# Prompt attention: from two query tiles of one head to one query tile of two heads

## The reference, cut to what matters

```python
p_c = masked_softmax(einsum('bqkgd,bnkd->bqkgn', q, kc) * scale, m_c)     # compressed keys, 63 of them
o_c = einsum('bqkgn,bnkd->bqkgd', p_c, vc)
p_s = masked_softmax(einsum('bqkgd,bkqmd->bqkgm', q, ks) * scale, m_s)    # selected: all tokens up to the query
o_s = einsum('bqkgm,bqkmd->bqkgd', p_s, vs)
p_w = masked_softmax(einsum('bqkgd,bwkd->bqkgw', q, kw) * scale, m_w)     # window: the last 512 tokens
o_w = einsum('bqkgw,bwkd->bqkgd', p_w, vw)
return gates[..., 0:1] * o_c + gates[..., 1:2] * o_s + gates[..., 2:3] * o_w
```

## Time and profile before

| | |
|---|---|
| time, median of 3 runs | 1833.09 us (1832.91 to 1834.04) |
| the profiled execution | 1833.64 us |
| its span from first to last instruction | 1831.9 us |
| granted TensorE clock, mean | 0.996 |
| PE / DVE / ACT / POOL busy | 98% / 64% / 51% / 25% of the span |

### The profile page before, as it was taken

How to read it: one execution, slowest core, us unless ns; L and a number is a source line. 1 busy time by engine, 2 the same in 40 slices (tenths; PEclk the granted TensorE clock), 3 DMA queues, 4 the chain that set the end, 5 groups by cost and what they waited for, 6 DMA issues and landing times.

```text
span 1831.9 us, 32124 instructions
## 1 busy us (share of the span) xinstructions
PE 1804.1 (98%) x11818; PEld 1618.9 (88%) x11819; DVE 1181.5 (64%) x1673; ACT 934.2 (51%) x1574; POOL 460.3 (25%) x627
## 2 busy tenths in 40 slices
PE   8999999999999999999999999999999999999998
PEld 8999999789999978999989999998768888888884
DVE  5744434566131279999999999645486686645756
ACT  4334343103021178888998888311133675545746
POOL 0000000000000016555555554002112444422431
PEclk9999999999999999999999999999999999999999
DMA  5233334314241550000000000525257797876875
GB/s 185 87 100 115 110 93 159 91 35 140 81 134 50 178 163 1 1 2 1 1 2 2 1 1 13 185 70 175 92 198 280 290 392 291 292 272 221 324 238 196
DMA packets 119762, 241.08 MB, mean 132 GB/s; under 512 B 27986, under 2 KB 84858, under 8 KB 113466
## 3 DMA queue, kind: packets, MB, share of 16 engines
q1 hardware_dynamic: 112666, 214.26, 33.4%
q0 software_dynamic: 6976, 25.17, 5.5%
HBM read 193.52 MB, written 45.88 MB: 131 GB/s over the span
## 4 chain that ended last, share of the span: by engine, by line
PE 57%; DVE 3%; ACT 2%; issue 1%; DMA 0%; POOL 0%; POOLq 0%; ACTq 0%; DVEq 0%
PE ps L3734 20%; PE ps L2191 7%; PE ps L2165 7%; PE ps L3316 4%; PE ps L263 4%; PE ps L2134 3%; PE ps L2136 3%; PE ps L3722 1%; PE ps L2126 1%; PE ps L3783 1%; PE ps L2210 1%; PE ps L2107 1%; PE ps L3728 1%; ACT region_w L2549 1%; PE ps L3793 0%
## 5 line engine op out<-in xcount | busy, mean ns | idle before, releaser
L2362 DVE TENSOR_REDUCE small<-ps 128x1 f32<-128x640 f32 (+7 forms) x256 | 176.3, 698 | 10.5 <-PE ps L2126 7.6
L2395 DVE TENSOR_TENSOR turned_low<-ps,turned_high 128x512 fp32r<-128x512 f32 (+2 forms) x304 | 178.0, 608 | 6.2 <-ACT turned_high L2562 4.5
L2562 ACT CAST turned_high<-ps 128x512 fp32r<-128x512 f32 (+2 forms) x304 | 155.4, 533 | 15.5 <-PE ps L2165 12.0
L2702 POOL TENSOR_SCALAR region_w<-region_w,small,gates 128x640 f32<-128x640 f32 (+7 forms) x172 | 138.4, 814 | 94.2 <-DVE small L2368 94.2
L2191 PE MATMUL ps<-turned_high,value_stacks 128*128 128x256 f32 (+1 forms) x608 | 159.2, 292 | 0.5 <-DVE turned_low L2395 0.5
L2191 PE MATMUL ps<-turned_low,value_stacks 128*128 128x256 f32 (+1 forms) x608 | 147.9, 281 | 0.0
L2134 PE MATMUL ps<-key_stacks,query_stacks 128*128 128x256 f32 (+3 forms) x384 | 141.0, 367 | 3.3 <-ACT region_w L2549 2.8
L3734 PE MATMUL ps<-down_parts,hidden_parts 128*128 128x512 f32 x552 | 131.1, 393 | 0.0
L2549 ACT ACTIVATE region_w<-ps,small 128x640 f32<-128x640 f32 (+7 forms) x172 | 121.2, 707 | 17.2 <-PE ps L2165 8.7
L3734 PE MATMUL ps<-up_parts,rows_parts 128*128 128x512 f32 x552 | 129.0, 389 | 0.1
L3734 PE MATMUL ps<-gate_parts,rows_parts 128*128 128x512 f32 x528 | 125.9, 394 | 0.0
(11 more groups left out here) (556 smaller groups left out, 4888.4 us busy)
## 6 DMA issues: line engine op xcount, KB each, us to landing
region_k<-in_w_gate SPq DMA_DIRECT2D x16, 2048.0 KB, 9.6
region_k<-in_w_up SPq DMA_DIRECT2D x16, 2048.0 KB, 10.9
region_w<-in_w_down SPq DMA_DIRECT2D x16, 2048.0 KB, 14.1
region_w<-in_w_in SPq DMA_DIRECT2D x14, 512.0 KB, 4.6
region_k<-in_w_in SPq DMA_DIRECT2D x10, 512.0 KB, 4.4
small<-gate_a SPq DMA_DIRECT2D x8, 516.0 KB, 3.5
region_w<-gate_b SPq DMA_DIRECT2D x8, 516.0 KB, 3.8
region_k<-in_x_prompt SPq DMA_DIRECT2D x8, 512.0 KB, 7.4
```

Of the source, the lines that this page charges most:

```text
L2362: nc.vector.tensor_reduce(nmax[:, n % 4:n % 4 + 1], sc, AX.X, ALU.max, negate=True).then_inc(s_max, 1)
L2395: nc.vector.tensor_tensor(lo, m.ps[:, turn_bank(G), 0:w], hi, ALU.subtract).then_inc(s_lo, 1)
L2562: nc.scalar.copy(hi, m.ps[:, turn_bank(G), 0:w]).then_inc(s_hi, 1)
L2702: nc.gpsimd.tensor_scalar(probs(H, t), probs(H, t), rec[:, H % 4, t:t + 1], m.gates[:, 2 * p + t, col:col + 1], ALU.mult, ALU.mult).then_i ...
```

## The change

A unit is now one query tile of two neighbouring heads 2J and 2J+1. The halves (u, g, a) stay 128, four to a unit, and the two jobs of a half are the two heads. Both have the same tile and so the same blocks; `runs`, `value`, `alone_ahead`, `first_value` and `ALONE_AHEAD` go, and `values` multiplies 256 columns for each block. A pass of the loop covers two heads, 8 units and 32 halves, and the tiles come in the order 0, 4, 1, 5, 2, 6, 3, 7. The queries of a unit, and its outputs in `RO`, are two pieces of 128 columns, 1032 columns apart. A compressed set is now two units (two tiles of two heads); both parts of its scores come behind the second job of the first of them; its clamps are needed in the sets with tile 0 alone, one in four instead of one in two. The gates are read accordingly. Buffers are laid out for the new widths. All four engines' orders are written out anew, for 32 halves per pass, so that all steps stand at other distances from each other than before. The unused `keep_awake` of this function goes.

```diff
-def queries_at(p, j):
-    return slice(j * NTOK + p * 256, j * NTOK + (p + 1) * 256), slice(p * 256, (p + 1) * 256)
+TILE_OF = (0, 4, 1, 5, 2, 6, 3, 7)
+def queries_of(x, u):
+    j, i = 2 * (u // TT), TILE_OF[u % TT]
+    return x.rearrange("p (j n) -> p j n", n=NTOK)[:, j:j + 2, i * P:(i + 1) * P]
+def two_heads(x):
+    return x.rearrange("p (t n) -> p t n", t=2)
+def query_slot(u):
+    return slice(u % 4 * 256, (u % 4 + 1) * 256)
...
-    NU = TT // 2 * NKV
-    NH2 = 2 * NU
-    NHALF = QPK * NH2
-    SCALED_BEHIND = (0, 7)
-    ALONE_AHEAD = (9, 10, 11, 12, 13, 14)
+    UNITS = QPK // 2 * TT
+    NHP = 4 * TT
+    NHALF = 4 * UNITS
+    SCALED_BEHIND = ((0, 1), (9, 1), (16, 1), (24, 1))
...
+    def tile_of(H):
+        return TILE_OF[H // 4 % TT]
+    def first_block(H):
+        return 0 if H % 2 == 0 else max(0, tile_of(H) - WBLK)
     def blocks(H):
-        j, p, g, a = half(H)
-        return [(b, t) for b in range(2 * p + 2) for t in range(2) if first_block(a, 2 * p + t) <= b <= 2 * p + t]
+        return [(b, t) for b in range(first_block(H), tile_of(H) + 1) for t in range(2)]
...
+    def clamped(c):
+        return TILE_OF.index(0) // 2 == c % (TT // 2)
...
-            for r, n in runs(H):
+            out = m.ps[:, 7, g * 256:(g + 1) * 256]
+            for n in range(width(H) // P):
                 for x in range(2):
-                    if (H, r, x) not in alone_ahead(H):
-                        last = value(H, r, x, n)
+                    last = nc.tensor.matmul(out, vs[:, a, g, first_block(H) + n, :], m.pt_parts[a][x][:, n * 256:(n + 1) * 256],
+                                            start=(a == 0 and n == 0 and x == 0), stop=False, skip_group_check=True)
...
-        for j in range(-1, QPK + 1):
-            at, c = NH2 * j, 2 * j
...
+        for j in range(-1, QPK // 2 + 1):
+            at, c = NHP * j, TT // 2 * j
+            scores(at + 8, 1)
...
+            turn(at + 33, 0)
+            scores(at + 36, 1)
+            turn(at + 34, 0)
+            values(at + 32)
+            scores(at + 37, 0)
+            values(at + 33)
+            scores(at + 37, 1)
+            scores(at + 38, 0)
+            turn(at + 35, 0)
+            values(at + 34)
+            turn(at + 36, 0)
...
```

More of the change, by code:

```diff
@@ L2073, in turned @@
         w = min(4, len(blocks(what)) - 4 * c) * P
[L2074 removed]
+        hi, lo = m.pt_parts[half(what)[2]]
         return w, hi[:, c * 512:c * 512 + w], lo[:, c * 512:c * 512 + w]
@@ L2147, in turn @@
             G = g_of[what, c]
-            between = alone_ahead(what - 1) if c == 2 and what != "C" else ()
             if what == "C":
@@ new lines, in _ @@
+            scores(at + 27, 0)
+            scores(at + 27, 1)
+            turn(at + 24, 1)
+            turn("C", c + 3)
+            values(at + 23)
+            scores(at + 28, 0)
+            turn(at + 25, 0)
+            turn(at + 25, 1)
+            scores(at + 28, 1)
+            turn(at + 26, 0)
+            values(at + 24)
+            turn(at + 26, 1)
+            scores(at + 29, 0)
+            values(at + 25)
+            scores(at + 29, 1)
+            turn(at + 27, 0)
+            turn(at + 27, 1)
@@ new lines, in _ @@
+            scores(at + 30, 0)
+            values(at + 26)
+            scores(at + 30, 1)
+            turn(at + 28, 0)
+            turn(at + 28, 1)
+            turn(at + 28, 2)
+            scores(at + 31, 0)
+            values(at + 27)
+            turn(at + 28, 3)
+            turn(at + 29, 0)
+            scores(at + 31, 1)
+            turn(at + 29, 1)
+            turn(at + 29, 2)
+            values(at + 28)
+            scores(at + 32, 0)
+            scores(at + 32, 1)
+            turn(at + 30, 0)
@@ L2315, in _ @@
+            scores(at + 39, 0)
+            values(at + 35)
+            turn(at + 36, 2)
+            scores(at + 39, 1)
+            turn(at + 37, 0)
+            scores(at + 40, 0)
     @block.vector
```

840 lines of the change are left out of this document (532 added, 308 removed).

## The result

The changed kernel takes 1836.7 us (median; 1834.6 to 1838.8) beside 1834.0 (1832.0 to 1835.9) for the kernel before: ratio 1.0013, interval 1.0007 to 1.0019. It is slower by 0.13%, with the interval clear of 1, and so within the 0.2% that the prediction called no change. The profiled execution has a span of 1835.0 us, where before had 1831.9.

A forecast was written before the change was run, and what follows sets the result against it. TensorE was taken to bound the attention stage, VectorE close behind. Values -8.6 us and new waits +3.6 us make -5.0: 1828.6 us profiled, 1828.1 us as median from 1833.1; range 1819 to 1837.

The forecast's parts named there:

- The values: TensorE's value matmuls: 320 narrow ones (128 columns) become 160 wide ones (256 columns), four narrow 0.34 us against two wide 0.236, saving 8.4 to 8.6 us.
- second rival: Nothing gained: columns alone set matmul price, or VectorE replaces TensorE as bound; 1830 to 1836 us, middle 1833; chance 0.25.
- VectorE's share: In mid prompt attention VectorE works 91 to 94% of the stage, 2 to 3 us of 58 behind TensorE.
- The new waits: Rewritten orders make TensorE wait for late engines between tiles 4 and 5: 0.9 us x 4 passes, 3.6 us lost.
- the walk: Both written orders summed beside each other, TensorE never waiting: none late before; after, worst 0.86 us at scores of half 39.
- The bound from the rows: Limits for TensorE's waits in the attention loop: -14 us if the old ones vanished, +14 if they doubled.
- The start: First units of the attention stage, with waits and lower clock: zero change, with 2 us to either side.
- The end: Last unit of the attention stage has 16, 10, 16, 10 blocks instead of 15, 10, 15, 10: under 1 us.
- The third: Rival: too little TensorE cover between small and large tiles, 16 times at 1 us each; slower, 1840 us; chance 0.1.
- The first rival: Equal work per unit removes old waits too: 1817.5 us if half go, 1821 if a quarter; chance 0.2.

## Why the prediction was wrong

Forecast 1828.1, range 1819 to 1837, measured 1836.7: the range holds it by 0.3 us, the forecast is 8.6 off, and the likeliest sign (faster, 0.55) was wrong; "same" had 0.34.

**The values: priced too low.** -8.6 us was priced; the distances give about 3.3 us a pass, some 13, and the run with the narrow ones back is 11.6 us longer. The step behind it took 0.17 us for a narrow pair "with what follows" and missed that a wide value matmul behind it takes 0.17 as well: 0.112 each, not 0.086. Of the 4.2 us a pass that this gives, transposes that had been cheaper beside value matmuls take 1.0 back. The half of the second rival by which columns alone set the price is refuted.

**VectorE's share: wrong.** 91 to 94% was worked out by taking 0.08 us of overlap off nearly every row and by shortest spacings. With the narrow matmuls left out it works 98.7% of a pass of 113.5, which is 97% of before's. Part of what was counted as cover is not there: in the trace of before, where a VectorE row waits for the one ahead of it, it starts some 0.03 us behind that one's end and not 0.08 ahead of it; with the waits for other engines the gaps add up to 5 us a pass. The engine was not 2 to 3 us of 58 behind TensorE but about level with it. How much that caps is shown by the same run: 8.0 us off TensorE gave 2.2. Of the 3.3 sought here it would have left about a quarter, if the rest of the sequence had stayed as it was; this figure is in proportion only, and was not measured.

**The new waits: the step that failed.** 3.6 us was charged for all four passes, 0.9 a pass at one late place. Measured are about 3.6 us in each pass, some 14 in four. The kind and the unit were right: in the unit of tile 4, a bank that ScalarE has not read. The place was off by one half: the longest wait, 0.80 us, is at half 38, and half 39, for which 0.86 was forecast, has 0.42. But the walk charged one place and dropped the others behind it, as though one shift cured them. The waits view has 17 of them in 3.5 passes, with 0.71 at half 46. The bound from the rows, +14 for doubled waits, was the better estimate. Why one wait is followed by others, I can only argue: a wait of TensorE makes the exponential behind its transposes late too, and so frees the next bank late. That the orders are the cause is shown by the rearrangement: the same units and work without most of these waits, 11.2 us faster. But the old units gained 6.9 us in the same way, and with the same narrow matmuls and orders of their own the new units stay 1.7 us a pass behind the old ones, so a part may belong to the units.

**The start: 1.7 us instead of 0 +- 2** in the first pass, from the lower clock, inside its bounds. Filling the gaps shows it. The end: 11.49 for 11.39 us from the last job to the last value and 0.53 for 0.30 us to the next stage, as small as said.

**The sum with the measured terms:** -13.2 + 14.4 + 1.4 (what the first pass loses beyond a steady one) + 0.1 = +2.7 us for the stage, beside +2.8 read from its ends and +2.7 between the medians. Against the forecast of -5.0 the waits are 10.8 us too many, and the values saved 4.6 us more than priced: that the time came out within the range owes something to luck, as these two errors oppose each other. The other 0.9 us of the 8.6 is the time before, 1833.1 in three executions and 1834.0 in seventeen.

**The rivals.** The second is the one that came true in what it would show: the pass still at 115.8 (116.0), with more waits for the other engines, 1836.7 against its 1830 to 1836. Its reason, VectorE in TensorE's place, is only half of it: with a fifth off VectorE's load after still has 115.0. The third, thin cover between a small and a large tile, has its place right: the longest waits are in the units of tiles 4 and 5. Its price was near as well, 4 us a pass for 3.6 measured, and its 1840 missed because the values brought more. The waits stand in front of scores, though, not of the first transposes. The first rival (old waits go too, 1817.5 to 1821) failed in the written orders; rearranged, the kernel comes nearer to it, 1825.5. VectorE's share was to rise by a point and fell by 1.4.

**What to carry over.** When two engines are nearly level, as here, a saving on one is worth little more than the distance to the other (8.0 us off TensorE gave 2.2), and that distance has to be measured by taking the work away, not by adding shortest spacings. When a change rewrites an in-order schedule, price the schedule first: here rearranging was worth 11.2 us in the new units and 6.9 in the old, and the wide matmuls 11.6. When waits are charged to the instruction ahead of them, take them out before reading what work was saved. Charge every late place of a walk until a second walk, with the first waits put in, shows that the later ones vanish.

## What was not expected of the hardware

- A 128-column matmul with its own weight load costs 0.112 us in a run of value matmuls and a 256-column one 0.118. The pair shows as 0.06 and 0.11, and the rest is in the row behind it (0.17 for 0.12), so a spacing must be read up to the second row behind a change of width.
- Behind a wait of 1.2 us and within one of 0.6 TensorE's clock fell to the lower level, from 683.8 to 694.0 us, with a further wait of 1.0 us in that stretch. Twenty added matmuls of 0.22 us in these gaps took 2.1 us off the first pass; the same twenty where the gaps lie elsewhere cost 4 us.
- VectorE rows overlap the next by 0.08 us only where the next one is free to start. Near the top its share in the windows is close to its load: at 389.0 of 400 us (97.3%) the listed waits are 1.3% of the time, and 383.7 (95.9%) meant some 3 points of slack, not 6 to 9.
